# Two-block transformer on one NeuronCore: retention sums of squares one block later, first wave reordered, two dot products moved

## The chip, the core and the metric

The kernel runs on one NeuronCore of a Trainium2 chip. The metric is the device time of one execution in microseconds (us): smaller is better. The engines are TensorE (PE; its weight loads are PEld), VectorE (DVE), ScalarE (ACT), GpSimd (POOL) and SyncE (SP). They run side by side and meet only through semaphores.

## The reference, cut to what matters

256 tokens of width 1024 pass through two models in turn. The first has two layers, each a token mixer and a gated feed-forward; the second has two hybrid layers, which the change doesn't touch. The parts that matter here:

```python
def first_block(x, c, ...):
    for layer in range(2):
        # six vectors of 1024 from one row c: shift, scale, gate (twice)
        shift_m, scale_m, gate_m, shift_f, scale_f, gate_f = split(silu(c) @ ada_w[layer] + ada_b[layer])
        h = rms_norm(x, g0) * (1 + scale_m) + shift_m
        y = attention_mixer(h) if layer == 0 else retention_mixer(h)
        x = x + gate_m * y
        h = rms_norm(x, g1) * (1 + scale_f) + shift_f
        x = x + gate_f * swiglu(h)

def retention_mixer(h):                    # 4 heads, q and k 256 wide, v 512 wide
    q, k, v, g = split(h @ w_in)           # 1024, 1024, 2048, 2048 columns
    q, k = rotary(q), rotary(k) / 16
    o = ((q @ k.T) * decay) @ v            # per head
    o = (o - mean(o)) * rsqrt(var(o) + 1e-5)
    return (silu(g) * (o * gn_gain)) @ w_o
```

## The kernel before, in words

**Weights in blocks.** All projection weights come as 444 blocks of 128x1024 fp32 through a ring of four slots. For block n SP loads `raw` (512 KB), ACT copies it rounded into `whi` (`hi(n)`, line 1083), DVE subtracts to get `wlo` (`lo(n)`, line 1540), and PE multiplies three times per 128x128 tile (hi by high half, hi by low half, lo by high half: lines 494 to 496), 24 matmuls a block. SP loads slot n%4 again when `lo` of the block in it is done; ACT's `hi(n)` also waits until PE has finished block n-4. Every engine's order of work is written out by hand; a wait on an engine holds back everything that stands behind it there. PE's results go to PSUM tiles (`gslot`, two of them in turn), which ACT or DVE must empty before PE may write the tile two further on.

**First wave (PE lines 693 to 719).** The first layer's shift and scale are made on PE from sixteen rows of `ada_w` (`adaw`, eight transfers of 1 MB): `ada_rows(half, vec)` waits for two of these transfers, ACT copies the result (`adrow`, line 1143), `ada_cols` turns it into a column, DVE adds the bias and normalises four of the eight tiles of h, ACT and DVE split these (lines 1151 and 1619). This happens for tiles 0 to 3 (half 0), then 4 to 7 (half 1). Meanwhile the first four weight blocks are multiplied by `run_first(tiles)` over pairs (k, n): k the tile of h, n the block. The order before is k by k: all four blocks for k = 0, then `ada_rows(1, 0)`, all four for k = 1, and so on. `keep_busy(n, bank)` (line 601) issues n matmuls of ones whose result nobody reads, 16, 6, 3, 30 and 8 of them at five places. Each fp32 matmul shows as two instructions.

**Attention stage (PE line 762, ACT 1202, DVE 1675).** 24 blocks. On DVE, iteration b does `lo(b + 3)` and, from b = 1 on, one dot product `ada_later(b - 1)` (line 1552, 128x1024), which makes one later column of shift, scale or gate from a row block `aw` that POOL loads (80 in all, five slots). At b = 5 and b = 9 `rope_moba` adds six 128x512 operations. From b = 12 on the heads' scores, minima and softmax weights come in. The output projection follows (`x_update`, line 1743, eight blocks), without dot products; the next 44 stand in the feed-forward that follows, the last 12 in the retention stage's blocks 17 to 31.

**Retention stage (PE line 847, ACT 1288, DVE 1815).** 48 blocks: 16 for q and k, 16 for v, 16 for the gate g. `RET_PARTS` hangs the work of head n on the gate blocks: part 0 (scores: PE `ret_scores`, DVE multiplies by the decay into `rp`) at block 32 + 4n, part 1 (PE `ret_out`; ACT squares into `sq[4:8]` and copies into `sq[0:4]`) at 33 + 4n, part 2 (DVE adds the four squares into one tile) at 34 + 4n, part 3 at 35 + 4n. Part 3 is a chain over three engines: PE `ret_sum` (one matmul with ones, line 845), ACT logarithm and exponential (after loading their table set), DVE four scalings and the product with silu(g) (lines 1796, 1799), ACT high half (1286), DVE low half (1801). On ACT and DVE, `hi` and `lo` of block b + 4 stand ahead of the parts of block b. ACT's own work on a gate block is a Silu (line 1301), whose table set has to be loaded again after part 3. `ret_out` of the next head waits for `rp`, and for ACT's copy of the head before.

Of the kernel before, what the change touches and what calls it, by code (L numbers as in the profile page):

```python
# [27 lines left out]
KT = D // P  # L28
# [10 lines left out]
B_ATT_O = B_QKV + 24  # L39
# [11 lines left out]
G_ATT_O = 24  # L51
# [63 lines left out]

RET_PARTS = {}
for _n in range(4):
    for _part, _b in enumerate((32, 33, 34, 35)):
        RET_PARTS[_b + 4 * _n] = (_n, _part)


RET_DOTS = [b for b in range(17, 32) if b % 4]


# [59 lines left out]
def build(nc, a, out):  # L184
# [8 lines left out]
    with ctx:  # L193
# [28 lines left out]
        S = ctx.enter_context(nc.psum_tensor("S", [P, 3, 512], fp32))  # L222
# [252 lines left out]
        def _(pe):  # L475
# [109 lines left out]
            def run_first(tiles):  # L585

                for k, n in tiles:
                    if n == 0:
                        pe.wait_ge(hi_ready, k + 1)
                        pe.wait_ge(h_ready, k + 1)  # L590
                    if k == 0:
                        pe.wait_ge(w_lo, n + 1)
                    o = first_tile(n)
                    wh, wl = whi[:, n, k * P:(k + 1) * P], wlo[:, n, k * P:(k + 1) * P]
                    pe.matmul(o, wh, h[:, k, 0:T], start=(k == 0), stop=False)
                    pe.matmul(o, wh, h[:, k, T:2 * T], start=False, stop=False)
                    ins = pe.matmul(o, wl, h[:, k, 0:T], start=False, stop=(k == KT - 1))
                    if k == KT - 1:
                        ins.then_inc(blk_done, 1)

            def keep_busy(n, bank):

                for _ in range(n):
                    pe.matmul(bank[:, 0:P], ones[:, :], ones[:, :], start=True, stop=True)  # L606
# [84 lines left out]


            pe.wait_ge(in_ones, 16)
            keep_busy(16, S[:, 0, :])
            for k in range(KT):
                sum_squares(0, k)
            pe.wait_ge(silu_c, 1)
# [3 lines left out]
                ins = pe.matmul(G[:, n, :], ones[0:1, :], cs[0:1, 512 * n:512 * n + 512], start=True, stop=True)  # L701
            ins.then_inc(cs_wide, 1)
            ada_cols(0, 0)
            keep_busy(6, S[:, 0, :])
            ada_rows(0, 1)
            keep_busy(3, S[:, 0, :])
            ada_cols(0, 1)
            keep_busy(30, S[:, 0, :])
            pe.wait_ge(cs_copied, 1)
            run_first([(0, n) for n in range(4)])  # L710
            ada_rows(1, 0)
            run_first([(1, n) for n in range(4)])
            ada_cols(1, 0)
            run_first([(2, n) for n in range(4)])
            ada_rows(1, 1)
            run_first([(3, n) for n in range(4)])
            ada_cols(1, 1)
            keep_busy(8, Tp[:, 0, :])
            run_first([(k, n) for k in range(4, 6) for n in range(4)] + [(k, n) for n in range(4) for k in range(6, 8)])

            def sb_scores(hh):
                g = 13 + 2 * (hh // 2)
# [91 lines left out]
            def ret_scores(hh):  # L814
                if hh == 0:
                    pe.wait_ge(rope_ready, 4)
                else:
                    pe.wait_ge(r_pt, hh)
                for o, r in ((0, slice(0, T)), (T, slice(P, T))):
                    for half in range(2):  # L820
                        kk = rqk[:, 8 + 2 * hh + half, P if o else 0:T if o else P]
                        q = rqk[:, 2 * hh + half, r]
                        ins = pe.matmul(S[:, 0, o:o + r.stop - r.start], kk, q, start=(half == 0), stop=(half == 1))
                ins.then_inc(r_sc, 1)

            def ret_out(hh):
                pe.wait_ge(r_pt, hh + 1)
                pe.wait_ge(rv_ready, hh + 1)
                if hh == 0:
                    for g in range(G_RET + 28, G_RET + 32):  # L830
                        pe.wait_ge(slot_free[g % 4], taken(g))
                else:
                    pe.wait_ge(r_of, hh)
                for m in range(4):
                    o = S[:, 1 + m // 2, (m % 2) * T:(m % 2 + 1) * T]
                    c = 512 * hh + P * m
                    pe.matmul(o, rv[:, 0, c:c + P], rp[:, hh % 2, 0:T], start=True, stop=False)
                    ins = pe.matmul(o[:, P:T], rv[:, 1, c:c + P], rp[:, hh % 2, T:384], start=False, stop=True)
                ins.then_inc(r_o, 1)

            def ret_sum(hh):

                slot = use_t()
                pe.wait_ge(r_added, hh + 1)
                pe.matmul(Tp[:, slot, 0:T], ones[:, :], sq[:, 4, :], start=True, stop=True).then_inc(t_done, 1)

            for b in range(48):
                if b == 0:
                    run_two(B_RET, G_RET, 16)
                elif b // 16 == 1:  # L850
                    run_tokens(B_RET + b // 4 * 4, G_RET + b // 4 * 4, b % 4)
                elif b > 1:
                    run(B_RET + b, G_RET + b, 1, 8, of_h)
                if b in RET_PARTS:
                    hh, part = RET_PARTS[b]
                    if part == 0:
                        ret_scores(hh)
                    elif part == 1:
                        ret_out(hh)
                    elif part == 3:  # L860
                        ret_sum(hh)
            run_late(B_RET_O, G_RET_O, 16, 12, lambda m, k: yr[:, k, :], lambda k: pe.wait_ge(r_lo, k // 4 + 1))
            sum_of_squares(3)
            ffn(B_FFN1, G_FFN1, 3)
# [215 lines left out]
        def _(act):  # L1080
# [207 lines left out]
            for b in range(48):  # L1288
                g = G_RET + b
                if b // 16 == 1 and b % 4 == 2:  # L1290
                    act.wait_ge(tok_done, 2 + b // 4 - 3)
                    evac_tokens(g - 2, rv[:, :, (b - 18) * P:(b - 14) * P], 0, vsum[:, b // 4 - 4, :, :])
                act.wait_ge(blk_done, B_RET + b + 1)
                if b < 16:
                    act.activation(rqk[:, b, :], gslot(g), ACT.Copy, scale=1.0 if b < 8 else 256 ** -0.5)\
                       .then_inc(slot_free[g % 4], 1)
                elif b < 32:
                    if b % 4 == 3:
                        evac_tokens(g - 3, rv[:, :, (b - 19) * P:(b - 15) * P], 1, vsum[:, b // 4 - 4, :, :])
                else:  # L1300
                    act.activation(rg[:, b - 32, :], gslot(g), ACT.Silu).then_inc(slot_free[g % 4], 1)
                hi(B_RET + b + 4)
                if b in RET_PARTS:
                    ret_part(*RET_PARTS[b])
            x_squares(B_RET_O, 16, G_RET_O, two_each)
            root(3)
            norm_hi(24, 24, 72)
# [229 lines left out]
        def _(dve):  # L1537
# [18 lines left out]
            def ada_later(r):  # L1556

                dve.wait_ge(ada_raw[r % ADA_SLOTS], 16 * (r // ADA_SLOTS + 1))
                ada_dot(aw[:, r % ADA_SLOTS, :], 16 + r).then_inc(ada_done, 1)
# [115 lines left out]
            for b in range(25):  # L1675
                if b == 5:
                    dve.wait_ge(in_att, 64)
                if b == 12:
                    dve.wait_ge(in_const, 48)
                if b in (22, 24):  # L1680
                    for hh in range(2 * b - 44, 2 * b - 40):
                        minus_sums(hh)
                if 12 <= b < 20:
                    moba_minima(b - 12)
                if b in (15, 17, 19, 21):
                    o_split((b - 15) // 2)
                if b >= 1:
                    lo(b + 3)
                if 12 <= b < 20:
                    moba_normalise(b - 12)  # L1690
                if b in (15, 17, 19, 21):
                    for hh in (b - 15, b - 14):
                        slot = wait_s()
                        dve.tensor_tensor(zs[:, hh, :], S[:, slot, 0:384], sbm[:, :], ALU.add).then_inc(s_free, 1)
                if b in (5, 9):
                    rope_moba(b // 4 - 1)
                if b in (19, 23):
                    softplus(b // 4 - 4)
                if b >= 1:
                    ada_later(b - 1)  # L1700
            for p in range(4, 8):
                o_split(p)

# [36 lines left out]
            two_each = [2 * m + 1 for m in range(8)]  # L1740
            of_down = [-(-FT * (m + 1) // 8) - 1 for m in range(8)]

            x_update(B_ATT_O, 8, G_ATT_O, one_each, 2, 4)

            def ffn(b, g, later=()):
                for i in range(FT // 2):
# [68 lines left out]
            for b in range(48):  # L1815
                lo(B_RET + b + 4)
                if b in RET_DOTS:
                    ada_later(68 + RET_DOTS.index(b))
                if b in (20, 24, 28, 32):
                    centre(b // 4 - 5)  # L1820
                if b in (8, 16):
                    rope_ret(b // 8 - 1)
                if b in RET_PARTS:
                    ret_part(*RET_PARTS[b])
            x_update(B_RET_O, 16, G_RET_O, two_each, 8, 10)
            ah_base[0] = FT
            norm(4, 24, 24, col(modA, 0), col(mod, 72), [B_FFN1 + 3])
# [509 lines left out]
```

## Time and profile before

| | |
|---|---|
| time, median of 3 runs | 1515.5 us (1514.02, 1515.5, 1520.41) |
| the profiled execution, its own time | 1519.1 us |
| its span, first to last instruction | 1517.3 us |
| mean granted PE clock | 0.991 |
| busy: PE, DVE, ACT, POOL | 1476.3, 1039.2, 853.0, 83.6 us |
| DMA | 292.02 MB, mean 192 GB/s |

1.8 us of the profiled execution's time lie around its span. Times in the rows below are counted from the span's start. The ends of matmuls are modelled, so an idle time of PE is shown a little shorter than the distance that its starts leave; "L837" is line 837. The granted clock is 1.00 at 2.4 GHz and 0.50 at 1.2 GHz.

### The profile page before, as it was taken

What the parts mean: (1) busy time and instruction counts of PE and PEld (TensorE: products, weight loads), DVE (VectorE), ACT (ScalarE), POOL (GpSimd) and SP (SyncE); (2) the same over time, 40 slices, a digit from 0 to 9 for tenths busy, and PEclk for the clock granted to TensorE, in tenths of its full rate; (3) what the DMA queues carried; (4) which work ended last, traced back from release to release, by engine and by line L of the source; (5) the groups of instructions that cost most, each with busy time, mean ns of one, the idle gap of its engine ahead of it and who ended that gap; (6) DMA issues with size and microseconds to landing.
All of it is one profiled execution on the core that took longest, in us unless ns stands there. A gap on an engine that the chain in (4) does not pass through costs nothing.

```text
span 1517.3 us, 30340 instructions
## 1 busy us (share of the span) xinstructions
PE 1476.3 (97%) x11662; PEld 1391.6 (92%) x11662; DVE 1039.2 (68%) x1833; ACT 853.0 (56%) x1452; POOL 83.6 (6%) x136
## 2 busy tenths in 40 slices
PE   9988999999998799999999999999999999999999
PEld 7777999999987799999998999889999898988999
DVE  2786788899695556555566856886667585687664
ACT  4446566544445555555555775565556676656553
POOL 0110000011000000000001000120000000021000
PEclk9999999999999999999999999999999999999999
DMA  9865489899674255655655455325666355533663
GB/s 366 308 232 189 127 291 291 291 362 334 199 281 134 84 162 160 190 182 188 186 193 184 133 161 179 106 91 176 189 195 218 119 167 159 162 98 97 196 194 126
DMA packets 81183, 292.02 MB, mean 192 GB/s; under 512 B 9185, under 2 KB 10465, under 8 KB 80946
## 3 DMA queue, kind: packets, MB, share of 16 engines
q1 hardware_dynamic: 68274, 244.31, 49.6%
q0 software_dynamic: 11792, 42.77, 8.4%
q10 hardware_dynamic: 1008, 3.41, 0.7%
q8 instruction: 79, 1.29, 0.3%
q14 instruction: 30, 0.25, 0.1%
HBM read 289.40 MB, written 1.05 MB: 191 GB/s over the span
## 4 chain that ended last, share of the span: by engine, by line
PE 88%; DVE 6%; ACT 3%; issue 2%; DMA 0%; SPq 0%; DVEq 0%; ACTq 0%
PE G L494 21%; PE G L496 21%; PE G L495 21%; PE G L553 2%; PE G L555 2%; PE G L554 2%; DVE wlo L1544 2%; PE O L1035 1%; DVE aw L1552 1%; PE S L1004 1%; PE Tp L960 1%; PE G L575 1%; ACT whi L1089 1%; PE Tp L888 1%; PE S L606 1%
## 5 line engine op out<-in xcount | busy, mean ns | idle before, releaser
L1544 DVE TENSOR_TENSOR wlo<-raw,whi 128x1024 fp32r<-128x1024 f32 x444 | 548.8, 1238 | 301.7 <-ACT whi L1089 299.1
L1089 ACT ACTIVATE whi<-raw 128x1024 fp32r<-128x1024 f32 x444 | 468.6, 1057 | 237.5 <-PE G L496 179.0
L494 PE MATMUL G<-h,whi 128*128 128x256 f32 x2096 | 598.7, 286 | 1.8 <-ACT mqk L1198 0.9
L495 PE MATMUL G<-h,whi 128*128 128x256 f32 x2096 | 583.5, 278 | 0.0
L496 PE MATMUL G<-h,wlo 128*128 128x256 f32 x2096 | 583.5, 278 | 0.0
L494 PEld LDWEIGHTS G<-h,whi 128*128 128x128 f32 x2096 | 397.2, 190 | 10.3 <-issue 5.9
L495 PEld LDWEIGHTS G<-h,whi 128*128 128x128 f32 x2096 | 395.8, 189 | 1.8 <-issue 0.5
L496 PEld LDWEIGHTS G<-h,wlo 128*128 128x128 f32 x2096 | 394.9, 188 | 0.0
L1552 DVE CUSTOM_DVE_ANT_0 aw<-aw,cs,cols 128x1024 f32<-128x1024 f32 x80 | 102.3, 1278 | 0.0
L494 PE MATMUL G<-ah,whi 128*128 128x256 f32 x352 | 98.0, 278 | 0.0
L495 PE MATMUL G<-ah,whi 128*128 128x256 f32 x352 | 98.0, 278 | 0.0
L496 PE MATMUL G<-ah,wlo 128*128 128x256 f32 x352 | 98.0, 278 | 0.0
L494 PE MATMUL G<-yh,whi 128*128 128x256 f32 x288 | 80.1, 278 | 0.0
L495 PE MATMUL G<-yh,whi 128*128 128x256 f32 x288 | 79.7, 277 | 0.0
L553 PE MATMUL G<-whi,h 128*128 128x512 f32 x192 | 77.7, 405 | 2.1 <-DVE wlo L1544 2.1
L496 PE MATMUL G<-yh,wlo 128*128 128x256 f32 x288 | 79.7, 277 | 0.0
L555 PE MATMUL G<-wlo,h 128*128 128x512 f32 x192 | 76.5, 398 | 0.0
L554 PE MATMUL G<-whi,h 128*128 128x512 f32 x192 | 76.3, 397 | 0.0
L470 POOL TENSOR_TENSOR bias<-dist,slopes 128x256 f32<-128x256 f32 (+1 forms) x48 | 38.9, 835 | 547.6 <-DVE mn L2074 539.5
L494 PEld LDWEIGHTS G<-ah,whi 128*128 128x128 f32 x352 | 66.8, 190 | 0.0
L495 PEld LDWEIGHTS G<-ah,whi 128*128 128x128 f32 x352 | 66.1, 188 | 0.0
L496 PEld LDWEIGHTS G<-ah,wlo 128*128 128x128 f32 x352 | 66.1, 188 | 0.0
(341 smaller groups left out, 2284.4 us busy)
## 6 DMA issues: line engine op xcount, KB each, us to landing
raw<-in_w SPq DMA_DIRECT2D x444, 512.0 KB, 3.8
aw<-in_ada POOLq DMA_DIRECT2D x80, 512.0 KB, 5.5
adaw<-in_ada SPq DMA_DIRECT2D x8, 1024.0 KB, 15.6
sn<-in_uq ACTq DMA_DIRECT2D x2, 768.0 KB, 4.2
x<-in_x SPq DMA_DIRECT2D x1, 1024.0 KB, 5.1
pt<-in_ukv ACTq DMA_DIRECT2D x2, 512.0 KB, 5.3
out<-x SPq DMA_DIRECT2D x4, 256.0 KB, 2.3
dec<-in_dec ACTq DMA_DIRECT2D x1, 512.0 KB, 4.1
```

The lines of the kernel that those rows point to most:

```text
L470: pool.tensor_tensor(bias[:, DIST[grp]], dist[:, DIST[grp]], slopes[:, c:c + 1].broadcast_to([P, w]), ALU.mult).then_inc(bias_ready, 1)
L494: pe.matmul(o, wh, mv[:, 0:T], start=(k == 0), stop=False)
L495: pe.matmul(o, wh, mv[:, T:2 * T], start=False, stop=False)
L496: ins = pe.matmul(o, wl, mv[:, 0:T], start=False, stop=(k == k_of - 1))
L553: pe.matmul(o, hh, wh, start=(k == 0), stop=False)
L554: pe.matmul(o, hl, wh, start=False, stop=False)
L555: ins = pe.matmul(o, hh, wl, start=False, stop=(k == KT - 1))
L575: pe.matmul(o[n], w[:, slot, k * P:(k + 1) * P], src[:, k, 0:T], start=(k == 0 and w is whi), stop=False)
L606: pe.matmul(bank[:, 0:P], ones[:, :], ones[:, :], start=True, stop=True)
L1089: act.activation(whi[:, s, :], raw[:, s, :], ACT.Copy).then_inc(w_hi, 1)
L1544: dve.tensor_tensor(wlo[:, s, :], raw[:, s, :], whi[:, s, :], ALU.subtract).then_inc(w_lo, 1)
L1552: return dve.tensor_tensor_reduce(out=w, in0=w, in1=cs[:, :], scale=1.0, scalar=cols[:, C_ADAB + n:C_ADAB + n + 1], op0=ALU.mult, op1=ALU.add,
```

## The change

The diff, whole:

```diff
--- before.py
+++ after.py
@@ -115,10 +115,11 @@
 
 RET_PARTS = {}
 for _n in range(4):
-    for _part, _b in enumerate((32, 33, 34, 35)):
-        RET_PARTS[_b + 4 * _n] = (_n, _part)
-
-
+    for _part, _b in enumerate((32, 33, 34, 36 if _n < 3 else 35)):
+        RET_PARTS.setdefault(_b + 4 * _n, []).insert(0 if _part == 0 else 1, (_n, _part))
+
+
+ATT_DOTS = [b for b in range(1, 25) if b not in (5, 9)]
 RET_DOTS = [b for b in range(17, 32) if b % 4]
 
 
@@ -691,7 +692,7 @@
 
 
             pe.wait_ge(in_ones, 16)
-            keep_busy(16, S[:, 0, :])
+            keep_busy(12, S[:, 0, :])
             for k in range(KT):
                 sum_squares(0, k)
             pe.wait_ge(silu_c, 1)
@@ -701,22 +702,24 @@
                 ins = pe.matmul(G[:, n, :], ones[0:1, :], cs[0:1, 512 * n:512 * n + 512], start=True, stop=True)
             ins.then_inc(cs_wide, 1)
             ada_cols(0, 0)
-            keep_busy(6, S[:, 0, :])
+            keep_busy(2, S[:, 0, :])
             ada_rows(0, 1)
-            keep_busy(3, S[:, 0, :])
+            keep_busy(2, S[:, 0, :])
             ada_cols(0, 1)
-            keep_busy(30, S[:, 0, :])
+            keep_busy(8, S[:, 0, :])
             pe.wait_ge(cs_copied, 1)
-            run_first([(0, n) for n in range(4)])
+            for n in range(2):
+                run_first([(k, n) for k in range(4)])
             ada_rows(1, 0)
-            run_first([(1, n) for n in range(4)])
+            run_first([(k, 2) for k in range(4)])
             ada_cols(1, 0)
-            run_first([(2, n) for n in range(4)])
+            run_first([(k, 3) for k in range(4)])
             ada_rows(1, 1)
-            run_first([(3, n) for n in range(4)])
+            keep_busy(2, Tp[:, 0, :])
             ada_cols(1, 1)
-            keep_busy(8, Tp[:, 0, :])
-            run_first([(k, n) for k in range(4, 6) for n in range(4)] + [(k, n) for n in range(4) for k in range(6, 8)])
+            keep_busy(6, Tp[:, 0, :])
+            for n in (0, 2):
+                run_first([(k, n + e) for k in range(4, KT) for e in range(2)])
 
             def sb_scores(hh):
                 g = 13 + 2 * (hh // 2)
@@ -852,13 +855,13 @@
                 elif b > 1:
                     run(B_RET + b, G_RET + b, 1, 8, of_h)
                 if b in RET_PARTS:
-                    hh, part = RET_PARTS[b]
-                    if part == 0:
-                        ret_scores(hh)
-                    elif part == 1:
-                        ret_out(hh)
-                    elif part == 3:
-                        ret_sum(hh)
+                    for hh, part in RET_PARTS[b]:
+                        if part == 0:
+                            ret_scores(hh)
+                        elif part == 1:
+                            ret_out(hh)
+                        elif part == 3:
+                            ret_sum(hh)
             run_late(B_RET_O, G_RET_O, 16, 12, lambda m, k: yr[:, k, :], lambda k: pe.wait_ge(r_lo, k // 4 + 1))
             sum_of_squares(3)
             ffn(B_FFN1, G_FFN1, 3)
@@ -1300,8 +1303,8 @@
                 else:
                     act.activation(rg[:, b - 32, :], gslot(g), ACT.Silu).then_inc(slot_free[g % 4], 1)
                 hi(B_RET + b + 4)
-                if b in RET_PARTS:
-                    ret_part(*RET_PARTS[b])
+                for hh, part in RET_PARTS.get(b, ()):
+                    ret_part(hh, part)
             x_squares(B_RET_O, 16, G_RET_O, two_each)
             root(3)
             norm_hi(24, 24, 72)
@@ -1696,8 +1699,8 @@
                     rope_moba(b // 4 - 1)
                 if b in (19, 23):
                     softplus(b // 4 - 4)
-                if b >= 1:
-                    ada_later(b - 1)
+                if b in ATT_DOTS:
+                    ada_later(ATT_DOTS.index(b))
             for p in range(4, 8):
                 o_split(p)
 
@@ -1740,7 +1743,7 @@
             two_each = [2 * m + 1 for m in range(8)]
             of_down = [-(-FT * (m + 1) // 8) - 1 for m in range(8)]
 
-            x_update(B_ATT_O, 8, G_ATT_O, one_each, 2, 4)
+            x_update(B_ATT_O, 8, G_ATT_O, one_each, 2, 4, later=(22, 23))
 
             def ffn(b, g, later=()):
                 for i in range(FT // 2):
@@ -1820,8 +1823,8 @@
                     centre(b // 4 - 5)
                 if b in (8, 16):
                     rope_ret(b // 8 - 1)
-                if b in RET_PARTS:
-                    ret_part(*RET_PARTS[b])
+                for hh, part in RET_PARTS.get(b, ()):
+                    ret_part(hh, part)
             x_update(B_RET_O, 16, G_RET_O, two_each, 8, 10)
             ah_base[0] = FT
             norm(4, 24, 24, col(modA, 0), col(mod, 72), [B_FFN1 + 3])
```

In words: part 3 of heads 0, 1 and 2 goes from block 35 + 4n to block 36 + 4n, behind part 0 of the next head; head 3 keeps it at block 47. `RET_PARTS` becomes a list for each block, and PE, ACT and DVE walk it. In the first wave the dummy matmuls become 12, 2, 2, 8, 2 and 6, and `run_first` takes k = 0 to 3 of block 0, then of block 1, then (after `ada_rows(1, 0)`) of block 2, then (after `ada_cols(1, 0)`) of block 3; the second half does k = 4 to 7 of blocks 0 and 1 by turns, then of blocks 2 and 3. On DVE, iterations b = 5 and b = 9 have no dot product; the remaining ones keep their order, so that 22 stand in the attention stage, and numbers 22 and 23 stand behind `lo` in the first two blocks of the output projection.

## Rows read from the trace of the kernel before

**Rows 1.** The page: busy time of each engine, and the chain that ended last

```profile
PE 1476.3 (97%) x11662; PEld 1391.6 (92%) x11662; DVE 1039.2 (68%) x1833; ACT 853.0 (56%) x1452; POOL 83.6 (6%) x136
...
PE 88%; DVE 6%; ACT 3%; issue 2%; DMA 0%; SPq 0%; DVEq 0%; ACTq 0%
```

**Rows 2.** Waits of PE over the whole span: total, times, longest

```profile
PE S L837 <- DVE rp L1787: 11.0, 4, 3.4
...
PE Tp L845 <- DVE sq L1791: 4.4, 4, 1.1
```

**Rows 3.** Timeline of PE in the retention stage: start, us, instruction, idle before it

```profile
465.80 0.70 PE L837 MATMUL S<-rp,rv 128*128 128x256 f32 x2 [0.79 <-DVE rp L1787]
...
475.26 0.67 PE L845 MATMUL Tp<-sq,ones 128*128 128x256 f32 x2 [1.12 <-DVE sq L1791]
...
486.20 1.22 PE L837 MATMUL S<-rp,rv 128*128 128x256 f32 x2 [3.40 <-DVE rp L1787]
```

**Rows 4.** The chain that ended last, heads 2 and 3, sum of head 3

```profile
509.27 1.22 PE S L837 x2
...
531.07 0.70 PE S L837 x2
...
540.62 0.67 PE Tp L845 x2
```

**Rows 5.** Timeline of ACT, head 0

```profile
468.72 1.03 ACT L1274 ACTIVATE sq<-S 128x1024 f32<-128x1024 f32 x1 [2.34 <-PE S L838]
...
471.46 0.38 ACT L1301 ACTIVATE rg<-G 128x256 f32<-128x256 f32 x1 [0.80 <-PE G L496]
...
474.18 0.38 ACT L1301 ACTIVATE rg<-G 128x256 f32<-128x256 f32 x1 [1.39 <-PE G L496]
...
475.52 1.28 ACT L1280 ACT_TABLE_LOAD   x1
...
480.65 1.06 ACT L1286 ACTIVATE yr<-sq 128x1024 fp32r<-128x1024 f32 x1 [3.00 <-DVE sq L1799]
```

**Rows 6.** Timeline of DVE, head 0

```profile
473.97 0.69 DVE L1790 TENSOR_TENSOR sq<-sq 128x512 f32<-128x512 f32 x1
...
477.69 1.67 DVE L1796 SCALAR_TENSOR_TENSOR sq<-sq,cols,rstd 128x256 f32<-128x256 f32 x4 [0.92 <-ACT rstd L1284]
...
484.39 1.22 DVE L1544 TENSOR_TENSOR wlo<-raw,whi 128x1024 fp32r<-128x1024 f32 x1 [1.41 <-ACT whi L1089]
```

**Rows 7.** Granted clock in three stretches: busy us per engine, PEclk, DMA share, GB/s

```profile
17.30:20.60 3.30, 3.30 (x19) 3.08 (x22) 2.00 (x6) 0.42 (x1) 0.00 (x0) 0.50 1.04 411
...
484.90:491.70 6.80, 5.50 (x18) 4.75 (x18) 2.38 (x4) 0.68 (x1) 0.00 (x0) 0.50 0.50 154
...
49.20:77.10 27.90, 23.34 (x150) 20.08 (x148) 27.66 (x38) 13.41 (x21) 4.23 (x8) 1.00 0.86 314
```

**Rows 8.** Timeline of PE in the first wave

```profile
12.77 1.92 PE L632 MATMUL Tp<-adaw,silcb 128*32 128x512 f32 x16
...
24.10 6.95 PE L606 MATMUL S<-ones 128*128 128x128 f32 x60
...
38.12 1.92 PE L632 MATMUL Tp<-adaw,silcb 128*32 128x512 f32 x16
...
41.50 0.95 PE L647 MATMUL S<-ones,adrow 128*128 128x1 f32 x8
```

**Rows 9.** Weight loads of PE, second half of the first ada_rows

```profile
13.22 0.13 PEld L632 LDWEIGHTS Tp<-adaw,silcb 128*32 128x32 f32 x4 [0.30 <-DMA adaw<-in_ada]
```

**Rows 10.** POOL, which waits for the last of the eight transfers of adaw

```profile
34.92 2.79 POOL L453 DMA_DIRECT2D aw<-in_ada  x5 [34.47 <-DMA adaw<-in_ada]
```

**Rows 11.** DVE, lo of the first four blocks

```profile
27.16 4.63 DVE L1544 TENSOR_TENSOR wlo<-raw,whi 128x1024 fp32r<-128x1024 f32 x4 [0.40 <-ACT whi L1089]
```

**Rows 12.** Groups of DVE from 49.2 to 77.1 us: the dot products

```profile
L1552 DVE CUSTOM_DVE_ANT_0 aw<-aw,cs,cols 128x1024 f32<-128x1024 f32 x9 | 11.5, 1277 | 0.0
```

**Rows 13.** Groups of DVE in the output projection, 159.3 to 179 us

```profile
L1544 DVE TENSOR_TENSOR wlo<-raw,whi 128x1024 fp32r<-128x1024 f32 x7 | 8.6, 1225 | 4.6 <-ACT whi L1089 4.6
```

## The prediction

> **What bounds the kernel now.** I read the page first: PE is busy for 97% of the span and carries 88% of the chain that ended last, DVE 6% [rows 1]. So time can come only from places where PE waits, runs at half clock, or does work that nobody needs. The list of PE's waits shows the first place: `ret_out` waits 11.0 us in four times for `rp` from DVE, and `ret_sum` 4.4 us in four times for the added squares [rows 2]. The timeline of PE then shows what one head costs: the starts of `ret_out` of heads 0 and 1 lie 486.20 - 465.80 = 20.4 us apart, with 1.12 us idle ahead of `ret_sum` and 3.40 us ahead of the next `ret_out` [rows 3]; the next heads follow after 23.1 and 21.8 us [rows 4]. The rows of ACT and DVE say why [rows 5, 6]: after `ret_sum` (475.26) ACT loads a table (475.52), makes the root, waits 3.00 us for DVE's scaling and product, copies (480.65), and only behind all that, and behind another table load, stand Silu and `hi` of block 36, behind these DVE's `lo` (484.39), and behind `lo` the new head's `rp`. The long chain of the old head stands in front of the short one that PE needs.
>
> The clock rows come next [rows 7]: from 484.9 to 491.7, right after the 3.40 us stall, PE was granted 0.50. From 49.2 to 77.1 DVE is busy for 27.66 of 27.90 us: there DVE is the bound. For the first wave I read PE's timeline from the start [rows 8 to 11].
>
> **Retention, part 3 one block back.** New order at block 36: scores of head 1, DVE's `rp`, and only then part 3 of head 0. Nothing is added; the same instructions move, and no DMA issue among them. PE's work for a head, without its two idles, is 20.40 - 1.12 - 3.40 = 15.9 us [rows 3]. A block takes 474.18 - 471.46 = 2.7 us (two Silus in step with PE) [rows 5], four of them 10.9; `ret_out` some 2.7 (465.80 to about 468.5, where ACT's squares follow it at 468.72) [rows 3, 5]; 2.3 are left for scores and sum.
>
> Can the other engines keep this pace? Count from T, the start of `ret_out` of head n+1, so that the block ahead of part 3 has ended at T - 5.0. ACT: Silu and `hi` 1.3 (T - 3.7), table 1.28 (T - 2.4), logarithm and exponential 0.9 (T - 1.5). DVE: `lo` and `rp` are done at about T - 1.9, 1.9 us before PE needs `rp`; then scalings 1.67 and product 1.2 (T + 1.3). ACT: copy 1.06 (T + 2.4), table 1.3, Silu and `hi` 1.3 (T + 5.0), squares and copy 2.0 (T + 7.0), Silu and `hi` of the next block 1.3 (T + 8.3). DVE: `lo` 1.2 and adding 1.1, so the squares are added at T + 10.6 (durations: [rows 5, 6]). PE comes to the next `ret_sum` only at T + 2.7 + 3 x 2.7 + scores 1.4, about T + 12.2. So both waits go, with 1.6 us to spare. The tightest place is the PSUM tile of the block behind the squares, freed at T + 7.3 and wanted at T + 8.1.
>
> Head 3 keeps its sum at block 47, where it can't be covered: PE is there at T + 8.4, the squares at T + 10.6. Before, the sum started 540.62 - 531.07 = 9.55 us behind that `ret_out` [rows 4]. What is late next is thus this one sum, by 2.2 us instead of 1.1. The whole: before 540.62 - 465.80 = 74.8 us [rows 3, 4]; after 3 x 15.9 + 10.6 = 58.3; **16.5 us less**. A stall of 2.2 us may cost a stretch at half clock. The nearest row is the 6.8 us at 0.50 behind the 3.40 us stall [rows 7], the other end is nothing; I charge half of it, 3.4 us at half speed, 1.7 us: **-14.8**, between -10 (ACT's tight place costs 1.5 us a head) and -17.
>
> **First wave.** Its end is set by PE's own queue, dummies included, and by what lands. Cutting the first 16 dummies to 12 is nearly covered: the second half of `ada_rows(0, 0)` had its weight load released by the transfer at 13.22 [rows 9]. 6 to 2 dummies, and 30 to 8 (6.95 us for 30, so 1.9 for 8 [rows 8]), let the rest come earlier. Block 0 then waits only for its own `lo`: the four of them took 4.63 us [rows 11], and before, PE was kept busy until all four were done. What becomes the limit is the last transfer of `adaw`: POOL was released by it at 34.92 [rows 10], so the second half of `ada_rows(1, 1)`, which ran about 0.9 us behind 38.12 [rows 8], can move by 39.0 - 34.9 = 4.1 us and no more. Between it and `ada_cols(1, 1)` stood block work until 41.50, 1.5 us behind its end; now ACT's copy sets 0.8: 0.7 us. Six dummies for eight behind `ada_cols`: some 0.4. And with two blocks by turns, block 0 ends with its 21st matmul instead of its 30th, at 2.7/24 = 0.11 each: 1.0 us. Sum 6.2 us until `hi(4)` and `lo(4)`, from which DVE's full stretch starts; the loads of blocks 4 to 7 were behind `adaw` in any case, and need to be there at 42 instead of 48.
>
> The doubt is the clock. From 17.3 to 20.6 PE ran at 0.50, behind a stretch with `ada_rows`, one-row and one-column matmuls [rows 7, 8]. The change leaves more such thin stretches, and an idle of some 2 us ahead of block 0. Half speed ahead of the last transfer hides behind it; behind it, it doesn't. I charge one stretch of 3.4 us, 1.7 us: **-4.5**, between -1 (only the reordering counts) and -6.5. The Trainium skill, "TensorE: Matmul & The Clock Gate", Part 1, says "the default state is throttled, and activity releases the throttle". By that rule dummies are not waste, and cutting them speaks against this edit; with two stretches the term would be -2.8, with none -6.2, and rows 7 show one in the first wave as it was.
>
> **Dots out of two blocks.** In DVE's full stretch [rows 7] each dot takes 1.2 us (nine took 11.5 with their overlaps) [rows 12], and both that are left out lie on the path to the first softmax weights, for which PE waits: **-2.4**. From b = 12 on there is one dot a block as before. Dots 22 and 23 now stand behind `lo` in the output projection, where DVE waited 4.6 us over seven blocks for ACT [rows 13], 0.66 a block: 1.2 us too much in each of two blocks is made up two blocks later, x of the third block is 1.2 us late, and PE wants that PSUM tile a block later still. I cost it at nothing; without that cover up to 2.4 us. The term lies between 0 and -2.6.
>
> **Sum.** -14.8 - 4.5 - 2.4 = -21.7 us. Against the profiled execution, 1519.1 - 21.7 = 1497.4; that execution stood 3.6 us above the median of the three shown, so for the median **1494**.
>
> **Rivals.** (1) *The front gives little.* PE falls to half clock behind the trimmed dummies, or the faster start meets the transfers: the DMA share was already 0.86 in DVE's full stretch, at 314 GB/s [rows 7], and `aw` and `raw` share it. Then only retention counts: -14.8 to -17, some 1500. Against it: DVE hardly waited there, and needs less than before.
>
> (2) *ACT becomes the bound of a head.* Its chain from T - 5.0 to T + 8.3 and the next Silu and `hi` fill 14.6 of 15.9 us. If hand-overs add 2 us, `ret_sum` and the PSUM tiles wait: some 2 to 3 us a head lost, -13 in all, 1502.
>
> (3) *The move does nothing.* The wait for `rp` only becomes a wait for the copy of the squares, because ACT must wait for the old head's low half there. Then -6.9 from front and dots, 1508.6: within 0.5%. Against it: the low half is done at T + 3.6, before ACT comes to the copy (T + 6).
>
> (4) *Slower: the clock stays down.* If the idle ahead of block 0 and the thin matmuls held PE at 1.2 GHz not for one stretch but through the attention stage's first twelve blocks, each block would take 5.4 us for 2.7, 32 us more, less the 4.6 us that PE stood idle there [rows 7]: +27, less 17 from retention and dots, +10, so 1526. It decides once half clock lasts over some 50 us. No row comes near: the longest is 6.8 us [rows 7].
>
> **How the numbers follow.** Forecast 0.73, (1) 0.11, (2) 0.09, (3) 0.05, (4) 0.02. The forecast's own range is 1489 to 1499. The range reaches from 1485 (no stretch at half clock lost, which gives 1490, and retention at its -17, and a median 2 to 3 us lower by chance: the three before lie 6 us apart) to 1503, where (1) and (2) lie, and leaves out less than 2 in 10. A change of 0.5%, 7.6 us, is about what a measurement of this kernel can tell from none. Faster by more: forecast, (1) and (2), 0.93; within: (3), 0.05; slower: 0.02.
>
> **What the profile after would show.** Retention right: `ret_out` starts 15.4 to 16.2 us apart, the waits of `ret_out` for `rp` near 1 us in all, one wait of 2 to 3 us at line 845, clock 1.00 between heads. Wrong: a wait of `ret_out` for ACT's copy, or of gate blocks for Silu. Front right: `ada_cols(1, 1)` at about 37, the first block of the loop's kind (L494) at about 45. Wrong: 0.50 behind 35 us. Dots right: the first transposes of the softmax weights 7 to 8.5 us earlier; wrong: DVE waiting for ACT between `lo`s there. The forecast falls if the time is above 1503.

## The result, and the profile after

| | before | after |
|---|---|---|
| time, median | 1514.76 us (4 runs, 1510.88 to 1520.41) | 1489.56 us (4 runs, 1485.9 to 1496.56) |
| profiled execution, its own time | 1519.1 us | 1496.56 us |
| span | 1517.3 us | 1494.7 us |

The ratio is 0.9839, 95% interval 0.9802 to 0.9876: 24.4 us less (18.8 to 30.0). 1494 us had been predicted, range 1485 to 1503. A repeat in a later series gave 1493.74 us against 1515.84 us, ratio 0.9848 (0.982 to 0.9877), so 22 to 25 us is the size of it. The profiled execution is the slowest of the four; why executions of one kernel lie this far apart is told in the last section.

The page of the changed kernel, answering to [rows 1], and its waits of PE over the whole span, answering to [rows 2]:

```profile
PE 1465.0 (98%) x11600; PEld 1380.3 (92%) x11600; DVE 1038.9 (70%) x1833; ACT 852.9 (57%) x1452; POOL 85.6 (6%) x136
...
PE 90%; DVE 5%; ACT 3%; issue 2%; DMA 0%; SPq 0%; DVEq 0%; ACTq 0%
```

```profile
PE Tp L848 <- DVE sq L1794: 3.2, 1, 3.2
...
PE G L596 <- DVE wlo L1547: 2.4, 1, 2.4
...
PE S L840 <- DVE rp L1790: 0.8, 1, 0.8
```

Lines have moved by 1 to 3. The 11.0 us in which `ret_out` waited for `rp` are 0.8, the four waits at `ret_sum` are one of 3.2 us (head 3), and there is a new one: block 0 of the first wave waits 2.4 us for its own `wlo`.

PE's timeline in the retention stage, answering to [rows 3, 4]: the starts of `ret_out` (L840) and of the last `ret_sum` (L848), with the wait ahead of it.

```profile
466.52 0.70 PE L840 MATMUL S<-rp,rv 128*128 128x256 f32 x2 [0.78 <-DVE rp L1790]
...
481.91 0.59 PE L840 MATMUL S<-rp,rv 128*128 128x256 f32 x2
...
497.29 0.59 PE L840 MATMUL S<-rp,rv 128*128 128x256 f32 x2
...
512.68 0.59 PE L840 MATMUL S<-rp,rv 128*128 128x256 f32 x2
...
524.08 0.67 PE L848 MATMUL Tp<-sq,ones 128*128 128x256 f32 x2 [3.17 <-DVE sq L1794]
```

The distances are 15.4 us each where they were 20.4, 23.1 and 21.8. From the first `ret_out` to the last `ret_sum` it is 524.08 - 466.52 = 57.6 us for 74.8: 17.2 us, most of the whole.

The order on DVE, answering to [rows 6], shows the mechanism:

```profile
480.46 0.28 DVE L1790 TENSOR_TENSOR rp<-S,dec 128x128 f32<-128x128 f32 x1
481.13 1.67 DVE L1799 SCALAR_TENSOR_TENSOR sq<-sq,cols,rstd 128x256 f32<-128x256 f32 x4 [0.39 <-ACT rstd L1287]
...
492.75 0.42 DVE L1794 TENSOR_TENSOR sq<-sq 128x256 f32<-128x256 f32 x1
```

`rp` of head 1 is done at 480.7, 1.2 us before PE takes it (481.91), and the scaling of head 0 comes behind it. The squares of head 1 are added at 493.2, and PE comes for them at 494.1.

The granted clock (columns as in [rows 7]):

```profile
17.70:21.00 3.30, 3.30 (x17) 0.63 (x10) 1.43 (x4) 0.11 (x1) 0.00 (x0) 0.50 1.02 406
27.90:31.30 3.40, 3.40 (x18) 3.27 (x16) 2.24 (x2) 0.42 (x1) 0.00 (x0) 0.50 1.01 406
484.90:491.70 6.80, 6.80 (x62) 6.79 (x61) 3.27 (x3) 6.77 (x10) 0.00 (x0) 1.00 0.19 60
```

The kernel before had a second stretch at half clock in the retention stage, behind the next stall:

```profile
508.80:512.20 3.40, 2.93 (x9) 2.56 (x10) 1.54 (x3) 0.00 (x0) 0.00 (x0) 0.50 0.53 160
```

In the retention stage the half clock is gone with the stalls (1.00 from 484.9 to 491.7, where it was 0.50). So the 17.2 us have two main parts: the waits for `rp` and the squares fell from 15.4 to 4.0 us, which is 11.4, and 6.8 + 3.4 = 10.2 us at half speed are gone, which is about 5.1 by my estimate. In the first wave a second stretch at 0.50 has come, right behind the idle ahead of block 0.

The first wave on PE, answering to [rows 8], and DVE's `lo` of block 4, with which DVE's full stretch begins (49.23 before, seen in the chain that ended last):

```profile
22.45 2.03 PE L607 MATMUL S<-ones 128*128 128x128 f32 x16
...
26.88 0.36 PE L596 MATMUL G<-h,whi 128*128 128x256 f32 x1 [2.40 <-DVE wlo L1547]
...
37.11 1.92 PE L633 MATMUL Tp<-adaw,silcb 128*32 128x512 f32 x16
...
39.75 1.05 PE L648 MATMUL S<-ones,adrow 128*128 128x1 f32 x8
```

```profile
46.46 1.23 DVE L1547 TENSOR_TENSOR wlo<-raw,whi 128x1024 fp32r<-128x1024 f32 x1 [3.14 <-ACT whi L1092]
```

The dots, at the first transposes of the softmax weights on PE, which started at 85.47 before:

```profile
80.28 0.55 PE L690 MATMUL Tp<-ident,pr 128*128 128x128 f32 x3 [2.53 <-DVE pr L1675]
```

They start 5.2 us earlier: 2.8 from the first wave, 2.4 from the dots.

### The profile page after: what moved, and what is told of

Same layout as the page of the kernel before. It is cut to its first block, busy times and chain, and to the rows that moved or that the text cites. A ratio compares the mean times of both kernels' runs of the same rounds, so it can differ in the third digit from the quotient of the medians.

```text
span 1494.7 us, 30216 instructions
## 1 busy us (share of the span) xinstructions
PE 1465.0 (98%) x11600; PEld 1380.3 (92%) x11600; DVE 1038.9 (70%) x1833; ACT 852.9 (57%) x1452; POOL 85.6 (6%) x136
## 4 chain that ended last, share of the span: by engine, by line
PE 90%; DVE 5%; ACT 3%; issue 2%; DMA 0%; SPq 0%; DVEq 0%; ACTq 0%
PE G L495 22%; PE G L497 22%; PE G L496 22%; PE G L554 2%; PE G L556 2%; PE G L555 2%; DVE wlo L1547 2%; PE O L1038 1%; PE S L1007 1%; PE Tp L963 1%; PE G L576 1%; PE Tp L891 1%; DVE aw L1555 1%; ACT whi L1092 1%; PE G L582 1%
## 5 line engine op out<-in xcount | busy, mean ns | idle before, releaser
L1555 DVE CUSTOM_DVE_ANT_0 aw<-aw,cs,cols 128x1024 f32<-128x1024 f32 x80 | 102.2, 1277 | 0.0
## 6 DMA issues: line engine op xcount, KB each, us to landing
adaw<-in_ada SPq DMA_DIRECT2D x8, 1024.0 KB, 15.6
```

Of the source, the lines that this page charges most:

```text
L1555: return dve.tensor_tensor_reduce(out=w, in0=w, in1=cs[:, :], scale=1.0, scalar=cols[:, C_ADAB + n:C_ADAB + n + 1], op0=ALU.mult, op1=ALU.add,
```

## The experiments

My theory: the three parts add up, and the retention part is worth so much because `rp` of the new head now stands ahead of the old head's long chain on ACT and DVE. Rivals: the gain comes from `ret_sum` finding its squares ready; the parts at the front are lost again before the attention stage ends; the clock, not the queue, sets the first wave.

**Each part alone, on the kernel before.** `ret_only` has the two hunks of `RET_PARTS` and its three readers, `first_only` the first wave, `dots_only` the lists of dot products, each word for word as in the diff.

> Only the retention move; first wave and dot products as before. My theory (the move takes the long chain of the old head from in front of the new head's rp): the starts of ret_out 15.4 us apart for all four heads, from the first ret_out to the last ret_sum 57.5 us instead of 74.8, ratio about 0.989, 17 us less. If instead the whole gain of 25 us came mostly from the first 80 us of the kernel: less than 10 us here.

> Only the first wave. By the profile of the changed kernel lo of block 4 starts 2.8 us earlier than before (46.5 for 49.2) and the total falls by 2.8 us. The rival, that this gain is lost again before the attention stage ends, gives 0. The prediction's 4.5 would need lo(4) at 44.7.

> Only the two dot products moved. DVE is the bound from 49 to 85 us, so the first transposes come 2.4 us earlier and the total falls by 2.4 us; nothing is lost in the output projection. The rival, that ACT or the transfers of raw take over as the bound of that stretch, gives under 1 us there.

| kernel | median | ratio to before (1514.47 us) |
|---|---|---|
| ret_only | 1498.39 us | 0.9878 (0.9844 to 0.9912) |
| first_only | 1511.59 us | 0.9974 (0.9947 to 1.0001) |
| dots_only | 1511.57 us | 0.9975 (0.9950 to 1.0000) |

By the medians 16.1 + 2.9 + 2.9 = 21.9 us, against 22.1 for the whole on its repeat. By the ratios the parts are 18.5 + 3.9 + 3.8 = 26.2 us against 23.0, so these runs show that the parts add up only to within some 4 us. The retention part is clear; each of the other two is at the edge of what these runs can tell from nothing, so I read them in the profiles, where positions are sharper. In `ret_only` the first `ret_out` to the last `ret_sum` takes 57.7 us. From the start of `lo(4)` to the first transposes it is 36.2 us in the profiles of before, ret_only and first_only, and 33.8 us in after, after_again, fill, late_sum and fill_late: 2.4 us for the dots. In the profile of `dots_only` itself DVE also finishes the softmax weights 2.4 us sooner behind `lo(4)`, but PE reaches the transposes only 1.9 us sooner (84.52 - 50.17 = 34.35 us): it ran at 0.51 from 77.2 to 84.1 and was late itself.

The rival that the front's gain is lost again before the attention stage ends falls too. The norm behind that stage starts at 178.6 to 181.5 us in before, ret_only and ret_chain_first, and at 170.2 to 174.7 us in the five profiles with both front parts and no other change there (after, after_again, late_sum, ret_load, ffn_break).

In the output projection DVE takes the two dots late, and has its old wait back two blocks on. DVE's timeline of the changed kernel there:

```profile
157.91 1.28 DVE L1555 CUSTOM_DVE_ANT_0 aw<-aw,cs,cols 128x1024 f32<-128x1024 f32 x1
...
159.84 1.22 DVE L1547 TENSOR_TENSOR wlo<-raw,whi 128x1024 fp32r<-128x1024 f32 x1
...
162.42 1.23 DVE L1547 TENSOR_TENSOR wlo<-raw,whi 128x1024 fp32r<-128x1024 f32 x1 [0.63 <-ACT whi L1092]
```

**The order of the parts, `ret_chain_first`.** As `ret_only`, but at block 36 + 4n part 3 of the old head comes first:

```diff
-        RET_PARTS.setdefault(_b + 4 * _n, []).insert(0 if _part == 0 else 1, (_n, _part))
+        RET_PARTS.setdefault(_b + 4 * _n, []).append((_n, _part))
```

> Part 3 at block 36 + 4n as in the change, but ahead of part 0 of the next head on PE, ACT and DVE; first wave and dots as before. If the gain comes from the order (rp ahead of the chain), rp is late by the chain's DVE part, ret_out waits 4 to 5 us in three heads, and most of the 17 us is gone: 0 to 6 us less than before. If it came from the squares being ready when ret_sum wants them, the gain stays at about 15 us.

1518.98 us, ratio 1.0012 (0.9976 to 1.0048): none of the gain is left. Its waits of PE:

```profile
PE S L837 <- DVE rp L1787: 15.6, 4, 4.9
```

`ret_sum` waits only for head 3 here (1.1 us, its sum stands where it stood before); for the other heads the squares are ready. Yet nothing is won, because `rp` is late by more (15.6 us in all for 11.0). So the gain is that of the order. This run was a little worse than I expected (0 to 6 us less): each `ret_out` behind such a wait ran at half clock. The first pieces of `ret_out` of heads 1, 2 and 3 in its chain show it, 1.22 us where the first piece behind a wait takes 0.70 at full clock. The kernel before had this at heads 1 and 2 only [rows 3, 4], so here 20.5 us of the stage ran at half clock where 10.2 did:

```profile
488.26 1.22 PE S L837 x2
...
511.70 1.22 PE S L837 x2
...
535.36 1.22 PE S L837 x2
```

**How much room is left, `ret_load`.** The changed kernel with ACT squaring three times for each head:

```diff
+                    for _ in range(2):
+                        chain.link(act.activation(sq[:, 4:8, :], out4, ACT.Square))
                     act.activation(sq[:, 4:8, :], out4, ACT.Square).then_inc(r_sq, 1)
```

> The changed kernel with ACT squaring the retention output three times instead of once for each head: 2.1 us more on ACT. ACT has 0.94 us idle a head in the changed kernel's profile. By my account of the slack (ACT is next, by about 1 us) the starts of ret_out 1 to 3 stand 16.5 us apart for 15.4, the last sum is 2 us later still, and the first ret_out to the last ret_sum takes 62 to 63 us for 57.9. If ACT were covered by PE, as the rival that only rp counts has it: 57.9, or 60 from the last sum alone.

One execution, 1499.13 us. `ret_out` starts at 460.36, 475.74, 493.24 and 512.49, the last sum at 525.51: 65.2 us for the whole. The first distance is 15.4, as the squares of head 0 have no chain in front of them; the second is 17.5, all of the 2.1 us added and not the 1.1 that I had left over ACT's idle; the third, 19.3, has a stretch at half clock in it (0.51 from 504.9 to 508.4). The waits say what overran:

```profile
PE Tp L848 <- DVE sq L1796: 4.6, 1, 4.6
PE G L495 <- ACT rg L1306: 3.9, 2, 1.9
```

It is the PSUM tile: PE's gate blocks wait 1.9 us each for the Silu behind the squares. In the changed kernel that Silu ends at 489.90, and PE starts on the tile at 489.98: 0.1 us of room, and not the 0.9 of ACT's idle that I had counted on. So ACT is next in this stage, and more by its order than by its load, as I read it: it is idle elsewhere in the same head.

**The two halves of the first wave.** `first_dummies` has only the new numbers of dummies, `first_order` only the new order.

> The kernel before with only the numbers of dummies changed, order k by k as before. Read at the start of lo of block 4 (50.2 us in three profiles with the old first wave, 49.2 in a fourth; 45.0 to 46.5 in those with the new one). The block order gives 1.0 us at the end (21st matmul for 30th) and 0.7 ahead of the last ada_cols, so here lo(4) should start near 47.1. If the dummies give all of it: 45.5.

> The kernel before with only the order of the first wave changed, dummies as before. Twelve more matmuls then stand ahead of the second ada_rows (1.4 us), 1.7 us come back at the end: lo(4) near 49.8, against 50.2. If order alone gave the gain: 45.5.

Both from one execution each (1512.01 and 1516.69 us beside 1515.85 us). DVE's `lo(4)` in them, first_dummies ahead:

```profile
50.34 1.23 DVE L1545 TENSOR_TENSOR wlo<-raw,whi 128x1024 fp32r<-128x1024 f32 x1 [4.20 <-ACT whi L1090]
```

```profile
49.17 1.23 DVE L1545 TENSOR_TENSOR wlo<-raw,whi 128x1024 fp32r<-128x1024 f32 x1 [3.25 <-ACT whi L1090]
```

Against the 50.15 to 50.20 us of three profiles with the old first wave order alone gives 1.0 us, for 0.4 expected; against the 49.23 of the fourth it gives 0.1, so one execution doesn't show it. Dummies alone give nothing, and there I was wrong by 3.2 us. The clock in that run:

```profile
28.60:35.40 6.80, 6.16 (x26) 2.66 (x26) 1.60 (x2) 0.50 (x1) 0.69 (x1) 0.51 1.05 383
```

Two stretches at half speed follow the idle. Half of 6.8 us is 3.4, about all of the miss. `ada_rows(1, 0)`, in the middle of them, took 3.64 us for 1.92:

```profile
31.20 3.64 PE L632 MATMUL Tp<-adaw,silcb 128*32 128x512 f32 x16
```

Whether the old order provoked the second stretch (it also waits for the `wlo` of the later blocks, 0.5 us twice) or chance did can't be told from one execution.

**Filling the idle, and head 3's sum.** On the changed kernel: `fill` has 18 dummies for 8 ahead of block 0. `late_sum` takes PE's `ret_sum(3)` from block 47 into `run_late`, behind nine tiles of the output projection; `fill_late` has both.

```diff
-            keep_busy(8, S[:, 0, :])
+            keep_busy(18, S[:, 0, :])
```

```diff
+                        if between is not None and m == 0 and k == 8:
+                            between()
...
-                        elif part == 3:
+                        elif part == 3 and hh < 3:
                             ret_sum(hh)
...
-            run_late(B_RET_O, ..., lambda k: pe.wait_ge(r_lo, k // 4 + 1))
+            run_late(B_RET_O, ..., lambda k: pe.wait_ge(r_lo, k // 4 + 1), between=lambda: ret_sum(3))
```

> The changed kernel unchanged, beside the next three. Sum of its parts as measured alone (16.1, 2.9 and 2.9 us by the medians): 21.9 us less than before, ratio 0.986; if the parts help each other, 25 us, 0.983. In its profile the feed-forward stages run at 27 or 26 instructions of PE in 3 us, each execution anew, as in the six profiles so far.

> The changed kernel with 18 dummies instead of 8 ahead of block 0, which fill the 2.4 us in which PE waits for its wlo. If that idle is what put the clock at 0.50 for 3.4 us behind it, that stretch goes, lo of block 4 starts 1.7 us earlier against the adaw transfers and the total is 1.7 us less than the changed kernel. If the thin stretches (rows and columns of ada) decide, the 0.50 stays and so does the time.

> The changed kernel with PE's sum of head 3 behind nine tiles of the output projection (3.1 us of work) instead of ahead of it; ACT and DVE as they are. My theory (this sum is what is late next, by 3.2 us): the wait at ret_sum falls from 3.2 to under 0.5 us, and in its place PE waits about 1.2 us for the low half of head 3, 2 us less than the changed kernel. Rival: the wait only moves, the time stays.

> Both of the last two. If they are independent 3.7 us less than the changed kernel, ratio to the kernel before 0.981.

| kernel | median | ratio to before (1515.84 us) | `lo(4)` | first `ret_out` to the norm behind the projection |
|---|---|---|---|---|
| after_again | 1493.74 us | 0.9848 (0.9820 to 0.9877) | 44.98 | 105.1 us |
| fill | 1495.93 us | 0.9856 (0.9825 to 0.9886) | 45.24 | 105.0 us |
| late_sum | 1492.35 us | 0.9842 (0.9818 to 0.9867) | 45.45 | 102.2 us |
| fill_late | 1487.87 us | 0.9816 (0.9790 to 0.9842) | 44.42 | 101.9 us |

`late_sum`: the wait of 3.17 us is gone, and the one that I expected in its place is there:

```profile
530.39 0.39 PE L522 MATMUL G<-yr,whi 128*128 128x256 f32 x1 [1.12 <-DVE yr L1807]
```

The part from the first `ret_out` to the norm is 3 us shorter, in both kernels that have it; 2 were expected. The idle gives about those 2 (3.17 us less 1.12). The rest is part of the 1.6 us that a stretch at half speed costs: after_again and fill have one from about the start of their sum on (told below), and these two have none there. The totals don't separate late_sum from after_again.

`fill`: the clock stayed at 1.00 behind block 0's start, in both kernels that have it. But it did so in after_again too, with its 2.40 us idle. The two stretches, after_again ahead of fill:

```profile
27.00:30.40 3.40, 3.40 (x32) 2.98 (x36) 3.26 (x3) 1.44 (x2) 0.00 (x0) 1.00 1.03 412
```

```profile
27.30:30.70 3.40, 3.40 (x32) 2.97 (x36) 3.18 (x3) 1.36 (x2) 0.00 (x0) 1.00 1.03 413
```

So the same kernel has the half-speed stretch in one execution (after) and not in another (after_again), and it is worth 46.46 - 44.98 = 1.5 us. The expectation of 1.7 us less is not borne out by the time, and two profiles alone would not show that the dummies prevent the stretch. All fourteen together say more. In seven of them PE idles for 2.4 us ahead of block 0 (after, after_again, late_sum, first_only, ret_load, ffn_break, first_dummies), and six of the seven have a stretch at 0.50 that begins between 0.2 us ahead of block 0's start and 1.6 us behind it. In the other seven the old 30 dummies or the 18 fill that time, PE idles for 0.2 us at most, and none has a stretch there. So the stretch goes with that idle, though the idle doesn't always bring it. What it costs with the new first wave:

| stretches at 0.50 in the first 45 us | profiles | `lo(4)` |
|---|---|---|
| none | fill_late | 44.4 |
| one, from about 18.5 to 22 | after_again, fill | 45.0, 45.2 |
| one, from about 26 to 29.5 | late_sum, first_only, ffn_break | 45.45, 45.8, 45.8 |
| two | after, ret_load | 46.5, 46.5 |

`fill_late` has the lowest median of all, and in its own comparison takes 1.84% less than the kernel before; that it beats the changed kernel isn't shown, the intervals overlap.

## Why the prediction was right, step by step

**The sum**: -21.7 us predicted, 24.4 by the ratio and 22.1 by the medians of the repeat. Faster with 0.93. In the two profiles 17.2 + 2.8 + 2.4 = 22.4 us nearly make up the 22.6 by which the spans differ; that has luck in it, as each of the two has one feed-forward stage at the slower of two rates (last section). The terms, against the profiles:

**Retention, -14.8**: 17.2 us in the profile, 16.1 by the medians. The mechanism was right: `rp` ahead of the chain, shown by ret_chain_first. Three sizes were off. A head costs PE 15.4 us and not 15.9, 1.5 us over three heads: the 15.9 was the old distance less its idles, and an idle is shown shorter than what the stall costs (the matmul ahead of it shows 0.28 us where the next ones follow at 0.11, and the first piece of `ret_out` takes 0.70 us behind a wait and 0.59 without). The last sum came 11.4 us behind its `ret_out` for 10.6, 0.8 the other way; that wait is 3.2 us for 2.2. And the stretch at half clock that I charged behind it (1.7 us) is not in the profile of the changed kernel, but it is in two others. In after_again it begins 0.3 us behind the start of the sum:

```profile
520.20:523.60 3.40, 3.40 (x16) 3.26 (x15) 2.48 (x6) 0.80 (x2) 0.00 (x0) 0.50 0.70 217
```

From the first `ret_out` to the norm behind the projection all three take 105 us, and still the stretch was not free. The output projection runs at one of two rates at full clock, the slow one in after and the fast one in after_again (30 us out of each, after first):

```profile
534.00:564.00 30.00, 30.00 (x257) 30.00 (x256) 18.68 (x23) 15.84 (x19) 0.00 (x0) 1.00 0.63 205
530.00:560.00 30.00, 30.00 (x267) 30.00 (x266) 18.58 (x23) 15.85 (x19) 0.00 (x0) 1.00 0.66 204
```

From the last sum to the norm it takes 45.9 to 46.0 us at the fast rate with no stretch (dots_only, ret_chain_first, first_dummies), 47.6 to 47.7 at the slow rate with none (before, first_only, first_order, after), and 47.5 to 47.6 at the fast rate with one (after_again, fill). So the stretch costs 1.6 us, as charged, and what was unsure is only whether it comes; by chance the slow rate costs as much, and hid this.

**First wave, -4.5**: 2.8 us between the two profiles read so far. Over all profiles `lo(4)` starts at 49.2, 50.15, 50.17 and 50.20 with the old first wave, and at 45.0, 45.45, 45.8, 45.8, 46.46 and 46.5 with the new one (late_sum, ret_load and ffn_break have it unchanged): 4.3 us between the medians. The profile of before was early by 0.9 us, that of after late by 0.6. Measured from the old median the new one, fill and fill_late included, gives 4.3 to 5.2 us with one stretch at half clock (-4.5 predicted), 3.7 with two (-2.8) and 5.7 with none (-6.2): a stretch cost about 1 us here and not 1.7. PE's own queue bounded it, as predicted: `ada_rows(1, 1)` moved from 38.12 to 35.6 in after_again and 37.1 in after, short of the bound of 4.1 us that the last transfer sets. By the Trainium skill, "TensorE: Matmul & The Clock Gate", Part 1, the throttled clock is the default and activity lifts it; first_dummies agrees (0.51 for 6.8 us behind the idle, no gain at all), after_again has the same idle and no such stretch. The rule says what can happen; the price behind that idle was 0 to 3.4 us here. The sum of the part was right, but it stood for an average: which price a single execution pays was not predicted.

**Dots, -2.4**: 2.4 us on DVE in every profile, 1.9 of it on PE in dots_only, 2.9 by the medians; that nothing is lost in the projection, as costed, agrees with this but is within the noise.

**Rival 1** (the front gives little) fell: 4.3 + 2.4 = 6.7 us of front and dots are in the profiles. **Rival 2** (ACT the bound of a head) fell, but ret_load shows that it stood nearer than I thought: the tightest place was the one named, the PSUM tile behind the squares, with 0.1 us of room for the 0.8 of my account. The block ahead of part 3 ended 4.3 us ahead of the next `ret_out` (ACT takes it at 477.63, `ret_out` starts at 481.91) and not 5.0, so the whole chain came 0.7 us later; most of that is the half microsecond of stalls that was left in the 15.9. **Rival 3** (a wait for ACT's copy) fell, there is no such wait. **Rival 4** (the clock stays down) fell: the longest stretch in both profiles of the changed kernel is 3.4 us.

**Signs.** Those of the retention stage came as told, but for the last wait (3.2 us for 2 to 3). Two of the front missed: `ada_cols(1, 1)` started at 39.75 in after and 38.27 in after_again, not at about 37, and the first block of the loop's kind at 48.3 and 46.8, not at about 45. The transposes came 5.2 us earlier between the two profiles, for 7 to 8.5; against the 86.38 and 86.43 of ret_only and ret_chain_first it is 6.1 in after and 7.6 in after_again.

## What to carry to other kernels

Where several engines walk through a hand-written order, ask of each short operation that the bottleneck engine waits for what stands in front of it on its own engine. Putting a long chain of the last unit behind the short first step of the next one cost nothing and gave 16 to 17 us here, a third of it by my estimate from the half clock that came behind the old stalls, while the same move with the other order gave none. Price dummies by the clock as well as by their time: where taking them away left PE idle for 2.4 us, the next real work began at half speed in six profiles of seven. And when two executions take the same time over a stage, look whether they got there in the same way before calling a cost nothing.

## What I had not expected of the hardware

The feed-forward stages run at one of two rates, at a granted clock of 1.00 in both, with PE never idle and the same instructions. The kernel before, 100 us out of its first and out of its second feed-forward stage:

```profile
205.00:305.00 100.00, 100.00 (x885) 100.00 (x884) 80.82 (x110) 61.52 (x83) 9.50 (x18) 1.00 0.88 288
640.00:740.00 100.00, 100.00 (x851) 100.00 (x850) 55.90 (x69) 56.83 (x76) 0.00 (x0) 1.00 0.59 186
```

And the changed kernel, where the two have changed places:

```profile
205.00:305.00 100.00, 100.00 (x851) 100.00 (x851) 78.02 (x107) 57.91 (x79) 8.97 (x17) 1.00 0.85 278
640.00:740.00 100.00, 100.00 (x884) 100.00 (x884) 59.75 (x77) 58.58 (x79) 0.00 (x0) 1.00 0.63 192
```

885 matmuls against 851 in 100 us are 113.0 and 117.5 ns a matmul. A whole feed-forward with its down projection takes 185.8 us at the one rate and 192.4 us at the other, and everything behind the retention's projection 922.2 to 923.0 or 928.6 to 930.4 us (926.3 in ffn_break, below, with its added dummies). The two rates are not the feed-forward's alone: the retention's output projection is slow in six profiles of fourteen, at 1.6 us, in executions whose feed-forward behind it is slow or fast. Of the fourteen profiles (before, after and the twelve runs) each of the two stages is slow in five: both in two, the first alone in three, the second alone in three, neither in six: it looks like a draw for each stage and execution. That it has nothing to do with the change is likely but not shown: the first stage, which runs ahead of everything that the retention move touches, is slow in five of the eight profiles with that move and in none of the six without. Two such draws of 6.6 us can account for most of what one kernel's executions differ by (1485.9 to 1496.6 us after, 1510.9 to 1520.4 before). Half clock adds to it: from the first `ret_out` to the norm the five profiles with the old retention order take 118.4 to 125.7 us, while after, after_again and fill take 105.0 to 105.2. Both together are why the edits worth 2 to 3 us can't be read from times.

`ffn_break` asked when it is drawn: the changed kernel with one more dummy matmul in each turn of the feed-forward loop.

```diff
                 with pe.Fori(1, FT // 2) as i:
+                    keep_busy(1, S[:, 0, :])
                     run(b, g, 4, 8, of_h, b4=i, g4=i)
```

> The changed kernel with one dummy matmul of 128 columns ahead of each turn of the feed-forward loop (ten turns a stage, some 0.1 us each). In eleven profiles a feed-forward stage runs at one of two rates from end to end, 884 or 851 PE instructions in 100 us. If a rate is drawn whenever the stream of equal matmuls is broken, the turns of one stage mix and the rates lie between; if it is drawn only after PE was idle, each stage shows one of the two again.

One execution, 1497.01 us. Both stages ran at the fast rate from end to end (883 and 884 in 100 us), so a break in the stream hardly draws anew, twenty fast draws in a row being unlikely; that leaves the idle ahead of a stage, or that a break holds the fast rate, which one execution can't tell apart. What makes the 4.5 ns stays open.
